# Layer 0's shift and scale as fp32 matmuls of two columns, with the norm of x taken in parts

## The reference

```python
shift, scale, gate = jnp.split(jax.nn.silu(c) @ w_ada + b_ada, 3, axis=-1)
shift_c, scale_c, gate_c = jnp.split(jax.nn.silu(c_ctx) @ w_ada + b_ada, 3, axis=-1)
h = rms_norm(x, norm_g) * (1.0 + scale[:, None]) + shift[:, None]
h_c = rms_norm(ctx, norm_g) * (1.0 + scale_c) + shift_c
... = jnp.split(h @ w_in, IN_SPLITS, axis=-1)
```

## Time and profile before

| | us |
|---|---|
| median of 3 runs | 1923.2 (1922.72 to 1926.9) |
| the profiled execution | 1927.93 |
| its span | 1926.1 |
| TensorE matmul busy | 1799.3 (93%) |
| TensorE weight load busy | 1497.2 (78%) |
| VectorE busy | 1127.7 (59%) |
| ScalarE busy | 971.5 (50%) |
| GpSimd busy | 669.2 (35%) |

### The profile page before, as it was taken

The page is one execution under the profiler, slowest core; times in us unless marked ns, Lnnn a source line. Parts: engine busy times, 40 slices in busy tenths (PEclk is TensorE's granted clock), DMA queues, the critical chain, the costliest instruction groups (busy, mean ns, idle before and its releaser), DMA issues. The chain is left out here.

```text
span 1926.1 us, 27717 instructions
## 1 busy us (share of the span) xinstructions
PE 1799.3 (93%) x11060; PEld 1497.2 (78%) x11060; DVE 1127.7 (59%) x1610; ACT 971.5 (50%) x1297; POOL 669.2 (35%) x490
## 2 busy tenths in 40 slices
PE   6789996899999999999999978999798999999999
PEld 5678886898888888888788857878696787777777
DVE  5556495459667656553234255749759866465343
ACT  6657523336445455553653156753337564555661
POOL 0011421537743434453153000144346544433150
PEclk9899998999999999999999999999799999999999
DMA  7123224422221122233244213324222221212352
GB/s 300 34 77 110 72 72 146 133 67 59 95 77 44 55 72 75 82 104 116 89 129 163 96 54 96 98 78 121 78 67 66 77 66 55 72 50 91 106 186 87
DMA packets 76414, 178.86 MB, mean 93 GB/s; under 512 B 6464, under 2 KB 29312, under 8 KB 76160
## 3 DMA queue, kind: packets, MB, share of 16 engines
q1 hardware_dynamic: 34272, 122.46, 20.6%
q10 hardware_dynamic: 42016, 54.63, 8.3%
HBM read 156.00 MB, written 21.07 MB: 92 GB/s over the span
## 5 line engine op out<-in xcount | busy, mean ns | idle before, releaser
L506 PE MATMUL banks<-hH,wHs 128*128 128x512 f32 x1984 | 599.0, 364 | 46.9 <-DVE hL L474 20.5
L506 PE MATMUL banks<-hH,wLs 128*128 128x512 f32 x1984 | 582.8, 355 | 0.0
L506 PE MATMUL banks<-hL,wHs 128*128 128x512 f32 x1984 | 581.1, 355 | 0.0
L1973 POOL TENSOR_TENSOR wLs<-raw,wHs 128x512 fp32r<-128x512 f32 x272 | 410.8, 1536 | 465.2 <-ACT wHs L872 465.2
L506 PEld LDWEIGHTS banks<-hH,wHs 128*128 128x128 f32 x1984 | 327.0, 191 | 123.6 <-issue 26.1
L506 PEld LDWEIGHTS banks<-hL,wHs 128*128 128x128 f32 x1984 | 324.8, 191 | 55.5 <-issue 2.2
L506 PEld LDWEIGHTS banks<-hH,wLs 128*128 128x128 f32 x1984 | 324.6, 191 | 54.7
L872 ACT ACTIVATE wHs<-raw 128x1024 fp32r<-128x1024 f32 x210 | 219.7, 1053 | 219.4 <-DMA raw<-wstream 219.2
L1529 DVE SCALAR_TENSOR_TENSOR acc<-padc,vecs,acc 128x783 f32<-128x783 f32 (+1 forms) x240 | 294.6, 1281 | 0.0
L861 ACT ACT_TABLE_LOAD x180 | 230.9, 1283 | 30.2 <-issue 13.0
L906 ACT ACTIVATE Pa<-banks,stat 128x768 f32<-128x768 f32 (+1 forms) x80 | 64.6, 813 | 144.0 <-DVE stat L1467 144.0
(11 more groups left out here) (242 smaller groups left out, 2330.8 us busy)
## 6 DMA issues: line engine op xcount, KB each, us to landing
raw<-wstream SPq DMA_DIRECT2D x210, 512.0 KB, 3.6
araw<-wstream SPq DMA_DIRECT2D x16, 512.0 KB, 12.6
E<-g_rows ACTq DMA_DIRECT2D x16, 384.0 KB, 7.0
egb<-eg_rows ACTq DMA_DIRECT2D x20, 256.0 KB, 4.2
inb<-intra_rows ACTq DMA_DIRECT2D x20, 256.0 KB, 4.5
parked_logits<-sg ACTq DMA_DIRECT2D x13, 384.0 KB, 4.1
xs<-xT SPq DMA_DIRECT2D x8, 384.0 KB, 11.4
intra_rows<-E ACTq DMA_DIRECT2D x8, 384.0 KB, 3.1
```

The costliest lines, as they stand in the source:

```text
L506: last = pe.matmul(out[:, a:b], w, m[:, kt, a:b], start=(kt == 0 and j == 0), stop=(kt == kts - 1 and j == 2))
L1973: ins = pool.tensor_tensor(wL[w % RING][:, o:o + 512], raw[w % RING][:, o:o + 512], wH[w % RING][:, o:o + 512].bitcast(F32), ALU.subtract)
```

## The change

Layer 0's first eight pairs (shift and scale) are made in plain fp32 with the raw weights stationary and the two columns of `cs32` moving: per pair 2 x 8 matmuls of 128 x 2 (line 594 of the new kernel). The cast, the split, the copy to `adar` and the transposes are gone for them; VectorE adds the bias straight from the bank (`first_col`). Pairs come in the order 0, 4, 1, 5, 2, 6, 3, 7, so that two successive ones hold shift and scale of the same two tiles, and `gs` is made in four parts. x is loaded in three pieces (tiles 0 to 2, 3 to 5, 6 and 7) behind the first three pairs. `nh` becomes four items of two tiles, which in layer 0 stand between the last pairs in the list. Only the first of the four ring units is cast and split ahead of the last two tiles; the others follow after.

```diff
+FIRST_TILES = ((0, 1, 2), (3, 4, 5), (6, 7), (), (), (), (), ())
+FIRST_PAIR = (0, 4, 1, 5, 2, 6, 3, 7)
...
-    for t in range(KT):
-        out += [("ada", 0, t), ("nsum", 0, t)]
+    for v, t in enumerate(FIRST_TILES[:4]):
+        out += [("ada", 0, v)] + [("nsum", 0, i) for i in t]
+    out += [("ada", 0, 4), ("nh", 0, 0), ("ada", 0, 5), ("nh", 0, 1), ("nh", 0, 2), ("ada", 0, 6), ("ada", 0, 7), ("nh", 0, 3)]
     for l in range(DEPTH):
-        out += [("nh", l), ("gb", l)]
+        out += ([("nh", l, i) for i in range(4)] if l else []) + [("gb", l)]
...
-FIRST = [("ada", 0, m) for m in range(2 * KT)]
+FIRST = [("ada", 0, 2 * m + j) for m in FIRST_PAIR for j in range(2)]
...
             for it in ITEMS:
                 stage[0], k, l = it[0], it[0], it[1]
-                if k == "ada":
+                if k == "ada" and first_ada(l, it[2]):
+                    m = it[2]
+                    pair = ("adap", l, m)
+                    out = product(pe, pair, 4)
+                    pe.wait_ge(*done("cs32"))
+                    pe.wait_ge(*done("araw", 2 * m + 1))
+                    for j in range(2):
+                        for kt in range(KT):
+                            last = pe.matmul(out[:, 2 * j:2 * j + 2], araw[:, 2 * m + j, kt * P:(kt + 1) * P],
+                                             cs32[:, kt, :], start=(kt == 0), stop=(kt == KT - 1))
+                    last.then_inc(*tick("pe", "pe", pair))
+                elif k == "ada":
...
-            for t in range(KT):
-                if t == 1:
+            for v, tiles in enumerate(FIRST_TILES):
+                for m in (2 * v, 2 * v + 1):
+                    sp.dma_start(araw[:, m, :], wstream[m]).then_inc(*tick("ada_raw%d" % v, "araw", m, by=16))
+                got[("araw", 2 * v)] = got[("araw", 2 * v + 1)]
+                if tiles:
+                    x = slice(tiles[0], tiles[-1] + 1)
+                    sp.dma_start(xs[:, x, :], xT[:, x, :]).then_inc(*tick("x_tiles%d" % v, "xt", tiles[0], by=16))
...
-                    while first_ada(l, m) and first_hi[0] < min(m + 3, KT):
...
-                        act.activation(awH[:, i:i + 2, :], araw[:, 2 * v:2 * v + 2, :], ACT.Copy).then_inc(*tick("act", "ahi", v))
...
-                    if l == 0 and m == 6:
-                        ahead(UNITS[0])
+                    if first_ada(l, m):
+                        continue
...
                 elif k == "nsum":
+                    if l == 0:
+                        square_of_x(0, it[2])
...
                 elif k == "nh":
-                    for t in range(KT):
+                    if l == 0 and it[2] == 3:
+                        ahead(UNITS[0], 1)
+                    for t in (2 * it[2], 2 * it[2] + 1):
...
+            def first_col(v):
+
+                pair, m = ("adap", 0, v), FIRST_PAIR[v]
+                added.add(("adaT", 0, v))
+                dve.wait_ge(*done("pe", pair))
+                dve.tensor_tensor(ada[:, 0, 2 * m:2 * m + 2, :], place[pair][:, 0:4].rearrange("p (u c) -> p u c", u=2),
+                                  bc(vecs[:, 0, V_BADA + 2 * m:V_BADA + 2 * m + 2], 2), ALU.add).then_inc(*tick_read("dve", pair))
+                got[("ada", 0, v)] = got[("read", pair, 0)]
+                if v % 2:
+                    scales(0, slice(v - 1, v + 1), v)
...
                 elif k == "nh":
-                    dve.wait_ge(*done("gs", l))
+                    i = it[2]
+                    if l == 0 and i == 3:
+                        low(UNITS[0], 1)
+                    dve.wait_ge(*done("gs", l, KT - 1 if l else 2 * i + 1))
```

More of the change, by code:

```diff
@@ L241, in build @@
         names += ["park_out0", "park_out1", "leaf_out0", "leaf_out1"] + ["park_in%d" % i for i in range(4)]
-        names += ["ada_raw%d" % i for i in range(KT)]
+        names += ["ada_raw%d" % i for i in range(KT)] + ["x_tiles%d" % i for i in range(3)]
         names += ["g_out", "eg_out", "e_in0", "e_in1", "i_out0", "i_out1"]
@@ L592, in _ @@
                     pe.wait_ge(*done("csL"))
[L593 to L597, removed]
+                    pe.wait_ge(*done("csx0"))
                     for u in units_of(it):
@@ L625, in _ @@
                 elif k == "gb":
+                    if l == 0:
+                        pe.wait_ge(*done("con_in"))
                     unit(units_of(it)[0], "gb")
@@ L1449, in ada_col, with scales @@
                 got[("ada", l, m)] = got[("read", key, 0)]
[L1451 to L1456, removed]
+            def first_col(v):
[7 more added lines that the diff above has]
+                    scales(0, slice(v - 1, v + 1), v)
+            def scales(l, tiles=slice(0, KT), last=KT - 1):
+                dve.wait_ge(*done("ada", l, last))
+                dve.scalar_tensor_tensor(gs[:, l, tiles, :], ada[:, l, 8 + tiles.start:8 + tiles.stop, :], 1.0,
+                                         bc(vecs[:, l, V_NG + tiles.start:V_NG + tiles.stop], 2), ALU.add,
+                                         ALU.mult).then_inc(*tick("dve", "gs", l, last))
             def maxes(l, h, qt):
@@ L1538, in _ @@
                     m = it[2]
[L1539 to L1545, removed]
                     if l == 0 and m == 0:
@@ L1564, in _ @@
                             dve.tensor_scalar(nlam[:, v:v + 1], nlam[:, v:v + 1], -lam0, None, ALU.add).then_inc(*tick("dve", "nlam", v))
-                    if l == 0 and m == 6:
-                        low(UNITS[0], RING - 1)
+                    if first_ada(l, m):
+                        if m == 0:
+                            dve.wait_ge(*done("con_in"))
+                        first_col(m)
+                        continue
                     for u in units_of(it):
@@ L1572, in _ @@
                         ada_col(0, 11)
-                    if l == 0 and m == KT - 1:
-                        ada_col(l, m)
-                        scales(l)
                 elif k == "nh":
-                    dve.wait_ge(*done("gs", l))
+                    i = it[2]
+                    if l == 0 and i == 3:
+                        low(UNITS[0], 1)
+                    dve.wait_ge(*done("gs", l, KT - 1 if l else 2 * i + 1))
                     dve.wait_ge(*done("rsn", l))
-                    if l:
+                    if l and i == 0:
                         dve.wait_ge(*done("pe", ("wout", l - 1, KT - 1)))
-                    for t in range(KT):
+                    for t in (2 * i, 2 * i + 1):
                         for p, (a, b) in enumerate(segs(TOK)):
```

38 lines of the change are left out of this document (8 added, 30 removed).

## The result

| | before | after |
|---|---|---|
| median, us | 1922.96 (6 runs, 1917.31 to 1926.9) | 1932.2 (6 runs, 1928.79 to 1934.59) |
| ratio to before | | 1.005, interval 1.0032 to 1.0069 |
| the profiled execution, us | 1927.93 | 1930.51 |
| TensorE matmul busy, us | 1799.3 | 1822.7 |
| mean granted clock | 0.973 | 0.966 |

The change makes the kernel slower, by 9.2 us or 0.5%. That is 9.6 above the predicted 1922.6 and just outside the range (1932.0). Rival 4 had 1930.9.

What follows compares the result with a forecast made beforehand. TensorE was taken to bound the kernel up to the first projection's end: pairs, sums, VectorE's hand-over and the projection summed to 72.7 us, 0.6 before 73.28. Median 1923.2 less 0.6 gave 1922.6, range 1909 to 1932.

Steps and rivals of the forecast that it cites:

- Rival 4: Weight loads of the pairs: the whole load runs on the array clock, 0.216 us a half-clock step, 1930.9; chance 0.19.
- The sum: TensorE's work in its new order, added from the first pair to the first projection's end at 72.7 us.
- pair 0 (half clock): First shift and scale pair on TensorE, starting at 6.4 us: 5.4 us at half clock, to 11.8.
- three sums: Sums of squares of three x tiles behind the first pair, clock rising: 2.4 + 2.4 + 1.2 = 6.0 us.
- pairs 3 to 7: Last five pairs on TensorE: 4.4 us with the clock falling midway, then 21.6 at half clock, to 60.4.
- biases, scales, split: VectorE's work between the last pair and the first projection: 2.0 us with semaphores, to 62.4.
- `gb`: First projection unit on TensorE, from a half clock: two K tiles at 1.92 and six at 1.08, 10.3 us.
- the price of a step at half clock: One weight load with its two-column matmul in a pair: 0.17 us at half clock, 0.11 at full.
- the anchor: First projection's end in one profiled execution, 73.28 us; the forecast end, 0.6 earlier, was taken off the median 1923.2.
- Rival 1: Clock holds over the pairs, 3.5 us each from the second on; the norm binds, 1911.5; chance 0.26.
- Rival 2: Weight loads of the pairs cost 0.11 us at either clock; first projection ends at 65.6, total 1915.5; chance 0.08.
- Rival 3: Weight loads of the pairs are light, 0.06 us as for transposes; pairs keep up with DMA, 1904.4; chance 0.05.

Runs made afterwards that it cites:

- e9: The kernel before, unchanged, profiled once more: 1921.12 us, with the first projection ending at 70.46 us.

## Why the prediction was wrong

The sum, part by part (durations in us):

| part | forecast | measured |
|---|---|---|
| pair 0 begins | 6.4 | 6.2 |
| pair 0 (half clock) | 5.4 | 6.8 |
| three sums | 6.0 | 5.5 |
| pair 1 (full), three sums | 9.5 | 9.1 |
| pair 2 (full), two sums | 7.1 | 6.2 |
| pairs 3 to 7 | 26.0 | 31.6 |
| biases, scales, split | 2.0 | 1.8 |
| `gb` | 10.3 | 10.2 |
| `gb` ends | 72.7 | 77.35 |

**The step that failed** is the price of a step at half clock. I took 0.17 us, from 322.49 to 322.66, because "The first load after a wait has no long matmul in front of the next". That is only the first spacing of a row, behind an idle array. The steady spacing is 0.213. The changed kernel shows both. The first two loads of its pair 0 take 0.50 us together, as those at 322.49 in the earlier trace rows:

```profile
6.20 0.50 PEld L594 LDWEIGHTS banks<-cs,araw 128*128 128x128 f32 x2 [6.20 <-issue]
```

With 0.33 for the second they are 0.17 apart, and yet the mean of the pair's 32 steps is 0.213. Some 168 of the 256 steps ran at half clock (pair 0, and about 136 of the last 160), and 168 times 0.043 is 7.2 us; pair 0 and the last five are 7.0 over the forecast. The sums, priced too high by 1.8, gave part of it back. At full clock the first spacing (0.10) and the steady one (0.109) nearly agree, which is why the same reading served there.

The trace of the kernel before had a closer row than the one used. It has 16 fp32 loads with 128 moving columns at a granted 0.50, 3.40 us to the start of what follows, 0.213 a step:

```profile
360.21 3.56 PE L739 MATMUL banks<-egb,S 128*128 128x128 f32 x16 [5.30 <-POOL egb L2044]
363.61 0.61 PE L539 MATMUL banks<-vn,PM 128*128 128x128 f32 x4
```

```profile
360.10:362.10 2.00, 1.89 (x9) 1.92 (x10) 0.00 (x0) 0.00 (x0) 1.27 (x1) 0.50 1.00 379
```

It could not say whether the load or the 128 columns set that step, but the earlier trace rows, the same kind at full clock, had been taken as a bound for the load, and this is its partner at half.

**Rival 4** was this case: "the whole load runs on the array clock", 0.216 a step, 1930.9, and it "decides from 0.192 on". I held against it and explained its own evidence, steady loads 0.21 apart, by the 256-column matmuls. Both explanations fit those rows. The one that scales with the clock should have weighed more, as the sums (1.2 to 2.3 us) and the 256-column matmuls (0.12 to 0.21) about double. Its line from which it decides is also off by a little: 0.192 adds 3.9 us over 176 steps, and the 4.4 that it names need 0.195.

**The second miss** was the anchor. The sum stood against `gb`'s end in one execution, 73.28, and I took the difference, -0.6, from the median of others. In two more executions `gb` ended at 70.4. The rows that priced "two K tiles at 1.92 (71.36 to 73.28)" themselves showed the clock at half at the end of `gb`, behind five waits of 0.3 to 0.9 us for the norm. In e9 the clock stayed full through the like waits. Of the 9.6 us between 1922.6 and 1932.2, 4.65 are the sum, 1.9 are this (73.28 against the mean of 71.4), and about 3 stay open.

**What was right.** TensorE is the bound from pair 0 to `gb`, and the norm is hidden under it. The clock falls under the two-column pairs: the granted clock is 1.00 from 33.8 to 36, 0.50 from 38 to 65.4. Pairs 1 and 2, behind the sums, run at full. Rival 1, that the clock holds, falls for 2 columns. Padding makes it true: 1917 against its 1911.5, and 1911.07 with the split early. Rival 2, a load of 0.11 at either clock, falls by 0.213. Rival 3, light loads, falls for blocks of 128; two blocks of 64 by turns at full clock do take its 0.06 together. "With semaphores 2.0" measured 1.8.

## What to carry to other kernels

- Price a repeated TensorE step from a steady row at the clock it will have, not from the first instruction behind a wait. Where only full-clock rows exist, expect about double at half clock (here 1.95 times for full blocks, 1.8 for blocks of 64).
- A stretch of very narrow matmuls may cost its time twice. Here 64 moving columns in place of 2 cost 0.03 us a pair at full clock, kept the clock, and saved 13 us. Blocks of 64 stationary columns written by turns to the two halves of the output saved 23 us.
- To price an edit that moves a few us in one place, take more than one execution of the kernel before: here the end of its head wandered by 3.

## What was unexpected of the hardware

The same 64-column loads and narrow matmuls take 0.055 us a step by turns and 0.089 one half after the other (0.030 and 0.050 at full clock), while a 128-column step takes 0.213 and 0.109: half the columns make the step more than twice as short, and turns make it shorter again by 0.034 (0.020 at full clock). And 64 moving columns behind 128-column loads kept a full clock through five pairs but left pair 0 at half (7.06 us, one execution), where with 128 columns it rose within the pair (5.33 to 6.70 us in four executions).
